# Two transformer blocks on one core: the queries and keys of seven of eight attention heads transposed by VectorE's block transposes instead of by TensorE

## What is computed

```python
qb = rms_norm(fq.reshape(B, S, FOX_HEADS, FOX_HEAD_DIM), fox_q_g[i])   # x * rsqrt(mean(x*x) + 1e-6) * gain
kb = rms_norm(fk.reshape(B, S, FOX_HEADS, FOX_HEAD_DIM), fox_k_g[i])
...
s = jnp.einsum('bhqd,bhkd->bhqk', qi, kt) * scale
s = s + Fqi[..., None] - F[:, :, None, :]
s = jnp.where(kpos[None, :] <= qpos[:, None], s, -jnp.inf)
pr = jax.nn.softmax(s, axis=-1)
return jnp.einsum('bhqk,bhkd->bhqd', pr, vt)
```

## Time and profile before

| | |
|---|---|
| median of 3 runs | 2565.72 us |
| lowest, highest | 2565.67, 2566.07 us |
| profiled execution, its own time | 2565.53 us |
| its span, first to last instruction | 2563.8 us |
| TensorE matmul busy | 2552.6 us (100%) |
| VectorE busy | 1646.1 us (64%) |
| ScalarE busy | 1220.6 us (48%) |
| GpSimd busy | 69.4 us (3%) |
| granted TensorE clock, mean | 0.999 |
| fox heads in the trace | about 218 us to 378 us |

### The profile page before, as it was taken

One profiled execution on the slowest core, in us unless ns is written; L12 is line 12 of the kernel. 1 busy time (PEld: TensorE's weight loads), 2 busy tenths in 40 slices (PEclk: granted clock), 3 DMA queues, 4 the chain that ended last, 5 costly groups with the idle time before them and its releaser, 6 DMA issues.

```text
span 2563.8 us, 36178 instructions
## 1 busy us (share of the span) xinstructions
PE 2552.6 (100%) x12362; PEld 2160.7 (84%) x12362; DVE 1646.1 (64%) x2302; ACT 1220.6 (48%) x1545; POOL 69.4 (3%) x123
## 2 busy tenths in 40 slices
PE   9999999999999999999999999999999999999998
PEld 7889998888888888888887788888888888888887
DVE  5555668676666666555966656666757676664444
ACT  5545545555555544444554444444544444444433
POOL 2000000000000000001001100000000000000000
PEclk9999999999999999999999999999999999999999
DMA  7666656766666665666656556665666666666664
GB/s 221 189 176 168 162 180 189 200 188 188 188 188 189 188 193 187 198 196 202 197 168 194 155 186 192 195 192 183 197 192 189 197 192 194 192 195 196 203 194 156
DMA packets 359369, 483.80 MB, mean 189 GB/s; under 512 B 22984, under 2 KB 170640, under 8 KB 359024
## 3 DMA queue, kind: packets, MB, share of 16 engines
q1 hardware_dynamic: 352768, 476.13, 62.1%
q0 software_dynamic: 2112, 5.31, 0.8%
q10 hardware_dynamic: 4400, 1.19, 0.2%
HBM read 480.41 MB, written 2.14 MB: 188 GB/s over the span
## 4 chain that ended last, share of the span: by engine, by line
PE 96%; DVE 3%; ACT 1%; issue 0%; DMA 0%; SPq 0%; POOLq 0%; POOL 0%; DVEq 0%; ACTq 0%
PE acc L1611 24%; PE acc L1613 24%; PE acc L1612 24%; PE acc L1859 6%; PE acc L1866 3%; PE T L1859 3%; PE X L1859 3%; PE T L1866 2%; PE X L1866 2%; DVE wlo L918 1%; PE acc L1919 1%; PE acc L1918 1%; PE acc L1917 1%; DVE turned L943 1%; DVE hid L943 1%
## 5 line engine op out<-in xcount | busy, mean ns | idle before, releaser
L918 DVE TENSOR_TENSOR wlo<-raw,whi 128x1024 fp32r<-128x1024 f32 (+1 forms) x916 | 1100.4, 1205 | 777.1 <-ACT whi L516 774.6
L516 ACT ACTIVATE whi<-raw 128x1024 fp32r<-128x1024 f32 (+1 forms) x916 | 949.2, 1044 | 1038.5 <-PE acc L1613 775.6
L1611 PE MATMUL acc<-whi,xt 128*128 128x512 f32 (+1 forms) x1472 | 564.3, 383 | 1.9 <-DVE wlo L918 1.9
L1613 PE MATMUL acc<-whi,xt 128*128 128x512 f32 (+1 forms) x1472 | 559.1, 380 | 0.0
L1612 PE MATMUL acc<-wlo,xt 128*128 128x512 f32 (+1 forms) x1472 | 558.8, 380 | 0.0
L1611 PEld LDWEIGHTS acc<-whi,xt 128*128 128x128 f32 x1472 | 276.4, 188 | 49.3 <-issue 2.0
L1613 PEld LDWEIGHTS acc<-whi,xt 128*128 128x128 f32 x1472 | 276.3, 188 | 47.5
L1612 PEld LDWEIGHTS acc<-wlo,xt 128*128 128x128 f32 x1472 | 276.5, 188 | 47.0
L1611 PE MATMUL acc<-whi,ht_hi 128*128 128x512 f32 x616 | 239.8, 389 | 0.0
L1613 PE MATMUL acc<-whi,ht_lo 128*128 128x512 f32 x616 | 239.7, 389 | 0.0
L1612 PE MATMUL acc<-wlo,ht_hi 128*128 128x512 f32 x616 | 239.6, 389 | 0.0
(11 more groups left out here) (340 smaller groups left out, 2596.4 us busy)
## 6 DMA issues: line engine op xcount, KB each, us to landing
raw<-in_w_up_dram SPq DMA_DIRECT2D x176, 512.0 KB, 3.7
raw<-in_w_down_dram SPq DMA_DIRECT2D x176, 512.0 KB, 4.4
raw<-in_w_gate_up_dram SPq DMA_DIRECT2D x176, 512.0 KB, 4.3
raw<-in_w_in_dram SPq DMA_DIRECT2D x256, 256.0 KB, 3.4
raw<-in_w_out_dram SPq DMA_DIRECT2D x64, 512.0 KB, 4.4
raw<-in_w_in_dram SPq DMA_DIRECT2D x64, 512.0 KB, 3.7
raw<-in_w_in_dram SPq DMA_DIRECT2D x128, 192.0 KB, 3.0
raw<-in_w_ple_gate_dram SPq DMA_DIRECT2D x32, 512.0 KB, 4.8
```

Of the source, the lines that this page charges most:

```text
L516: act.activation(whi[:, s, :, 0:w.width], raw[:, s, :, 0:w.width], ACT.Copy).then_inc(hi_made, 1)
L918: dve.tensor_tensor(wlo[:, s, :, 0:w.width], raw[:, s, :, 0:w.width], whi[:, s, :, 0:w.width].bitcast(F32), ALU.subtract).then_inc(lo_made, 1)
L1611: pe.matmul(out_, h_, wh_, start=(j == 0 and kk == 0), stop=False)
L1613: done = pe.matmul(out_, l_, wh_, start=False, stop=(j == w.n - 1 and kk == KS - 1))
```

## The change

For heads 0 to 6 TensorE's four transposes go. VectorE does them instead, as 16 `transpose` instructions, each of one strip: 32 partitions by 128 elements (2 token tiles, q and k, 32 columns). Eight of them stand after stage 4, right behind `f_scale_qk`, and eight after stage 5. They write a new tile `fqkt_s` in SBUF, which takes the place of `fqt_s` and `fkt_s` at the same size. ScalarE multiplies the norm weights in place, reading and writing `fqkt_s`, still after stage 6. TensorE's scores now wait for the semaphore `f_qt`, which both of ScalarE's copies raise. Head 7 keeps TensorE's transposes and bank T1.

```diff
-        "fox": (FH // 2, 16, 2, (FH, FH, FH, FH)),
+        "fox": (FH // 2, 16, 2, (1, FH, FH, FH)),
...
-            def f_copy_qt(b):
+            def f_copy_qt(b, last=False):
                 act.wait_ge(f_turned, b + 1)
-                act.activation(fqt_s[:], bank[T1][:, 0:S], ACT.Copy, scale=gains[:, g_fq:g_fq + 1]).then_inc(f_qt, 1)
-                act.activation(fkt_s[:], bank[T1][:, S:2 * S], ACT.Copy, scale=gains[:, g_fk:g_fk + 1]).then_inc(bank_read[T1], 1)
+                q, k = (bank[T1][:, 0:S], bank[T1][:, S:2 * S]) if last else (fqkt_s[:, 0], fqkt_s[:, 1])
+                act.activation(fqkt_s[:, 0], q, ACT.Copy, scale=gains[:, g_fq:g_fq + 1]).then_inc(f_qt, 1)
+                act.activation(fqkt_s[:, 1], k, ACT.Copy, scale=gains[:, g_fk:g_fk + 1]).then_inc(f_qt, 1)
+                if last:
+                    act.wait_ge(f_qt, 2 * FH)
+                    act.sem_inc(bank_read[T1], 1)
...
+            def f_turn(b, half_):
+                if half_ == 0:
+                    dve.wait_ge(f_norm, b + 1)
+                row = fqk_s[:].rearrange("p t (j b c) -> p t j b c", j=2, c=B)
+                col = fqkt_s[:].rearrange("p j (t q r) -> p t j q r", t=T, r=B)
+                for q in (2 * half_, 2 * half_ + 1):
+                    for c in range(P // B):
+                        done = dve.transpose(col[B * c:B * c + B, :, :, q, :], row[B * q:B * q + B, :, :, c, :])
+                if half_:
+                    done.then_inc(f_turned, 1)
...
-                after = {3: [lambda: f_evac(b, w), lambda: f_meansq(b, w)], 4: [lambda: f_scale_qk(b, w)], 7: [lambda: f_row_bias(b)]}
+                after = {3: [lambda: f_evac(b, w), lambda: f_meansq(b, w)], 4: [lambda: f_scale_qk(b, w), lambda: f_turn(b, 0)],
+                         5: [lambda: f_turn(b, 1)], 7: [lambda: f_row_bias(b)]}
...
             def f_scores(b):
-                pe.wait_ge(bank_read[T1], USE0[T1]["fox"] + b + 1)
+                pe.wait_ge(f_qt, 2 * b + 2)
...
-                after = {4: [lambda: f_turn(b)], 6: [lambda: f_scores(b)]}
+                after = {6: [lambda: f_scores(b)]}
```

More of the change, by code:

```diff
@@ L239, in sandwich_kernel @@
         (yt_hi, yt_lo, wg_raw, wg_both, bias_bc, gl, lsx, crow, cols, em, rows_bc, mask_m, mask_f,
-         qk_s, v_s, so_s, qt_s, kt_s, dw_s, pt_s, y_s, f_s, fqk_s, fsq_s, fqt_s, fkt_s, fg_s, fp_s, fpt_s) = group([
+         qk_s, v_s, so_s, qt_s, kt_s, dw_s, pt_s, y_s, f_s, fqk_s, fsq_s, fqkt_s, fg_s, fp_s, fpt_s) = group([
             ("yt_hi", [P, KD, S], F32R), ("yt_lo", [P, KD, S], F32R),
@@ L250, in sandwich_kernel @@
             ("f_s", [P, 2, T, 3 * FD], F32), ("fqk_s", [P, T, 2 * FD], F32), ("fsq_s", [P, T, 2 * FD], F32),
-            ("fqt_s", [P, S], F32), ("fkt_s", [P, S], F32), ("fg_s", [P, S + P], F32),
+            ("fqkt_s", [P, 2, S], F32), ("fg_s", [P, S + P], F32),
             ("fp_s", [P, S + P], F32), ("fpt_s", [P, S + P], F32)], ctx)
@@ L705, in _ @@
             hi(ws[0], {1: [lambda: f_softmax(FH - 2)], 3: [lambda: f_evac(FH - 1, before), lambda: f_copy_pt(FH - 2)],
-                       4: [lambda: f_split(FH - 2), lambda: f_copy_qt(FH - 1)], 6: [lambda: f_softmax(FH - 1)],
+                       4: [lambda: f_split(FH - 2), lambda: f_copy_qt(FH - 1, True)], 6: [lambda: f_softmax(FH - 1)],
                        7: [lambda: f_copy_pt(FH - 1), lambda: f_split(FH - 1)]})
@@ L1775, in _, with last_turn @@
                 mlstm(h, False)
-            def f_turn(b):
-                pe.wait_ge(f_norm, b + 1)
-                free(T1, "fox", b)
+            def last_turn():
+                pe.wait_ge(f_norm, FH)
+                free(T1, "fox", 0)
                 for j in range(2):
@@ L1786, in f_scores @@
             def f_scores(b):
-                pe.wait_ge(bank_read[T1], USE0[T1]["fox"] + b + 1)
+                pe.wait_ge(f_qt, 2 * b + 2)
                 free(X1, "fox", b)
-                pe.matmul(bank[X1][:, 0:P], fqt_s[:, 0:P], fkt_s[:, 0:P], start=True, stop=True)
-                pe.matmul(bank[X1][:, P:P + S], fqt_s[:, P:S], fkt_s[:], start=True, stop=True).then_inc(f_scored, 1)
+                pe.matmul(bank[X1][:, 0:P], fqkt_s[:, 0, 0:P], fqkt_s[:, 1, 0:P], start=True, stop=True)
+                pe.matmul(bank[X1][:, P:P + S], fqkt_s[:, 0, P:S], fqkt_s[:, 1], start=True, stop=True).then_inc(f_scored, 1)
             def f_weights_turn(b):
@@ L1831, in _ @@
                      after={1: [lambda: f_weights_turn(FH - 2)],
-                            2: [lambda: f_output(FH - 2, 0), lambda: f_turn(FH - 1)], 3: [lambda: f_scores(FH - 1)],
+                            2: [lambda: f_output(FH - 2, 0), last_turn], 3: [lambda: f_scores(FH - 1)],
                             5: [lambda: f_weights_turn(FH - 1)]},
```

## The result

| | before | after |
|---|---|---|
| median | 2565.72 us | 2578.36 us (2578.15 to 2578.42, 5 runs) |
| ratio, with 95% interval | | 1.0049 (1.0038 to 1.006) |
| span of the profiled execution | 2563.8 us | 2576.7 us |
| VectorE busy | 1646.1 us | 1679.1 us |

The changed kernel is 12.6 us slower, where the prediction said 11.7.

A forecast was written before the change was run, and what follows sets the result against it. TensorE bounds the kernel before, VectorE heads 0 to 6 after. Head 0's 3.99 + 5 x 1.33 = 10.6 us, plus 1.11 for head 6's scores, gives 11.7: 2577.2, or 2577.4 us against the median; range 2570.5 to 2585.

The forecast's parts named there:

- Price of a strip: One new 32x128 VectorE transpose: 0.317 us without overlap, sixteen 5.1 us a head; bounds 0.20 and 0.45.
- size term: Part of a VectorE transpose's cost that depends on length: 134 ns less going from 256 to 128 elements.
- VectorE becomes the bound: In later heads, logits 11.12 us after the scaling instead of 9.79, next scaling 20.09 instead of 18.76: +1.33 a head.
- TensorE's stops: TensorE waits for low parts: 0.1 us at stage 5, 1.4 at stage 6; scores begin at 10.05 instead of 8.94.
- The walk: Timeline of one head from the start of `f_scale_qk`, before and after: next head at 20.09 us instead of 18.76.
- Head 0: First head: TensorE waits about 2.2 us for stage 5, 1.4 for stage 6; with ScalarE's table load, +3.99 us.
- rival 3: Pauses cost clock: one stage at 1.2 GHz in each head, 2.08 us each, 14.6 more, 2592 us; chance 0.03.
- The step that was short: The sum's term for the heads after head 0: 5 x 1.33 us, VectorE setting the pace.
- Rival 1: VectorE's transposes overlap, about 0.20 us each: later heads gain 0.44, net -1.1 us, 2564.6 us; chance 0.10.
- Rival 2: Length hardly matters to a VectorE transpose: 0.42 us each, +22.5 us, 2588 us; chance 0.08.
- Rival 4: More slack than walked: each head loses some 0.5 us less, +7 us or less, 2572 us; chance 0.17.

The follow-up runs named there:

- half-strip kernel: Changed kernel without the second eight strips of each head, half of q and k staying zero: median 2567.99 us, in two groups (2566.1 to 2566.4, 2567.8 to 2568.1).

## Why the prediction was right, step by step

- **Price of a strip**: 0.317 forecast, 0.315 to 0.316 measured. A strip is 303 ns long where the 32x256 form is 436, so the size term is 133 ns; 134 were taken from another operation. The choice between overlap and none was right too.
- **VectorE becomes the bound**: right. Logits 11.06 after the scaling (11.12 forecast), next scaling 20.01 (20.09).
- **TensorE's stops**: the one at stage 6 was 1.17 to 1.19 us of idle time, against 1.4. The one at stage 5 was 0.1 in heads 2, 4 and 6, as forecast, but 0.49 to 0.59 in heads 1, 3 and 5: the table load of the head before makes their scaling late but not TensorE, which is ready 3.8 us after the scaling in head 1 and 4.3 in head 2. The scores came at 10.18 after the scaling, not at 10.05. Most of these 0.13 us are in a restart: the first matmul after a stop stands 0.63 us ahead of the fourth (258.72 to 259.35), where it is 0.52 in an undisturbed stage. The walk priced a stop at its idle time alone. In the half-strip kernel with head 0 on TensorE the same two terms, 0.13 us of idle time ahead of stage 5 (273.39) and 0.1 for the restart, make most of the step from 18.31 to 18.56 us.
- **Head 0**: +3.99 forecast, +3.95 measured. The stop at stage 5 was 2.03 us (2.2 forecast); the one forecast for stage 6 didn't come (see rival 3), but VectorE's walk through copies and table load, which gave the 3.99, holds.
- **The step that was short**: 1.33 us for each of heads 1 to 5. It holds for heads 1, 3 and 5 (1.25 to 1.28) and not for 2 and 4 (1.90 and 1.89). I saw the table load in head 0 only, though it stands in every turn of ScalarE's loop, and a turn is two heads. Before, it ended well ahead of the scores and cost nothing; in the changed kernel the high part of the next stage waits behind it, and VectorE's low part waits for that. ScalarE, head 2 of the changed kernel:

```profile
282.07 0.83 ACT L516 ACTIVATE whi<-raw 128x768 fp32r<-128x768 f32 x1
282.92 1.28 ACT L516 ACT_TABLE_LOAD   x1
284.22 1.58 ACT L516 ACTIVATE whi<-raw 128x768 fp32r<-128x768 f32 x2
```

VectorE waits 0.54 us for it at the low part that follows, a wait that the heads without a load don't have:

```profile
285.10 0.96 DVE L922 TENSOR_TENSOR wlo<-raw,whi 128x768 fp32r<-128x768 f32 x1 [0.54 <-ACT whi L516]
```

Heads 2 and 4 together are 1.13 us over the forecast. The other heads are 0.2 under it, and the last scores and the first scaling 0.2 over: together 1.1 us, from the forecast's 11.75 (before rounding) to the 12.85 of the table.

- **Rival 1 (overlap)** was priced at 2564.6; with overlapping strips the run took 2564.60, and its head 0 came 1.97 us later (2.0 forecast). So its walk was sound; that the total agrees to 0.01 us is luck. The change of groups excluded it for the real kernel.
- **Rival 2 (length hardly matters)**: out, by the 303 ns for 128 elements against 436 for 256.
- **Rival 3 (clock)**: its mechanism exists, in one place and in a cheaper form. The prediction named a fall of the granted clock between 235 and 375 us as a sign that it is wrong, and this sign came. Its ground for expecting none, the 1.87 us pause that left the clock at 1.00, was a single execution; the stop of 1.80 us above shows that the same place can end either way. In head 0 of the changed kernel, after a stop of 2.03 us:

```profile
236.00:238.00 2.00, 0.05 (x1) 0.00 (x0) 1.95 (x5) 0.00 (x0) 0.00 (x0) 1.00 0.03 9
238.00:240.00 2.00, 1.92 (x7) 1.92 (x8) 1.89 (x8) 0.00 (x0) 0.00 (x0) 0.59 0.30 52
240.00:242.00 2.00, 2.00 (x8) 1.96 (x7) 1.52 (x3) 1.39 (x3) 0.00 (x0) 0.56 0.60 153
```

Stage 5 ran at half clock and ended at 241.84, when the low part of stage 6, begun at 240.61, was just ready: the slow stage took the place of the second stop and cost next to nothing. That the rival was cheap is therefore owed to VectorE being late anyway; in the half-strip kernel the same fall made stage 5 longer by 1.5 us (3.75 against 2.21), and nothing hid that. Stops of 1.2 us in the later heads left the clock at 1.00.

- **Rival 4 (more slack)** expected some 0.5 us less a head. Heads 1, 3 and 5 are 0.07 us below the walked 20.09, so there was hardly any.

## What to carry over

Work moved from the engine that bounds to an "idle" one must fit where it is put: follow the receiving engine's stream through one period, with its waits, and compare with the slack at the tightest point. A share of 64% says nothing of that. The load alone would have fitted (17.8 us of VectorE work a head under 18.3 us of TensorE's). With 2.2 us of VectorE's waits, which nothing covered, it did not. The same strips at other stages turned +12.6 us into 1.6 less than before, which can't be told from no change, and with head 0 left on TensorE into 2.8 less. And where a loop holds a hidden instruction such as a table load, count it in every turn.

## What the runs showed of the hardware

- A 32x128 f32 block transpose takes 303 ns and costs VectorE 0.315 us when its output (changed kernel) or its input (the run in which only the input's group changes) begins in another group of 32 partitions than that of the strip ahead, and 0.20 us (256 to 257 ns long) when neither changes.
- After a stop of TensorE of 2.04 us the granted clock fell to half for one stage (3.75 us instead of 2.21) in one execution and not in another of the same kernel. A stop of 1.80 us at the start was followed by half clock too, others of 1.87 and 2.02 us in the same place were not, so the length of the stop alone doesn't decide it.
- ScalarE's table load in the fox heads is 1.28 us long and came in each of the three turns of the loop. Where the first turn stood ahead of the loop, there was one load in all.
- A stop of TensorE costs about 0.1 us beyond its idle time (0.63 us to the fourth matmul instead of 0.52).
